# Two heads of scattered gate cells, in place of one, sent behind the first gathered expert rows

## The reference, cut to what matters

```
s1, s2 = scores of the query against two lists of 128 keys, per head (8 heads)
v1, i1 = top_k(s1, 16);  v2, i2 = top_k(s2, 16)
top_s, pos = top_k(all 256 sums, 16);  idx = i1 * 128 + i2   # one of 16384 experts
gate = softmax(top_s)
act  = gelu(x . expert_u[idx])
out += (gate * act) @ expert_v[idx]
```

## Time and profile before

| | us |
|---|---|
| median of 3 runs | 4127.82 (4125.06 to 4128.35) |
| the profiled execution | 4125.72 |
| its span in the trace | 4123.9 |
| PE busy | 3736.4 (91%) |
| DVE busy | 2646.7 (64%) |
| POOL busy | 1887.1 (46%), of it L2147 scatters 416.5 (256 of them) |

### The profile page before, as it was taken

The page is one execution under the profiler, slowest core; times in us unless marked ns, Lnnn a source line. Parts: engine busy times, 40 slices in busy tenths (PEclk is TensorE's granted clock), DMA queues, the critical chain, the costliest instruction groups (busy, mean ns, idle before and its releaser), DMA issues. The chain is left out here.

```text
span 4123.9 us, 42872 instructions
## 1 busy us (share of the span) xinstructions
PE 3736.4 (91%) x15498; PEld 2761.5 (67%) x15498; DVE 2646.7 (64%) x5548; ACT 749.7 (18%) x1387; POOL 1887.1 (46%) x1714
## 2 busy tenths in 40 slices
PE   8889999987899999995798899999878999999947
PEld 7546788876566666652685467888766666666516
DVE  4666214848777677776857662158387777768777
ACT  2244302211100000000222433022110000000002
POOL 6101102777555554566571011027775554555564
PEclk9889999998999999997897899999989999999978
DMA  3301144549999999999623011445499999999996
GB/s 106 113 21 45 52 141 139 143 113 309 408 409 408 409 396 410 403 409 407 239 84 113 31 42 56 141 138 143 111 328 409 409 404 409 404 410 407 404 398 238
DMA packets 331938, 1047.14 MB, mean 254 GB/s; under 512 B 78928, under 2 KB 95952, under 8 KB 312784
## 3 DMA queue, kind: packets, MB, share of 16 engines
q0 software_dynamic: 184320, 537.08, 35.6%
q1 hardware_dynamic: 130352, 488.45, 31.3%
q10 hardware_dynamic: 17056, 18.88, 1.3%
HBM read 1008.49 MB, written 35.78 MB: 253 GB/s over the span
## 5 line engine op out<-in xcount | busy, mean ns | idle before, releaser
L1681 PE MATMUL bank<-v_tile,shared 128*128 128x512 f32 x2048 | 906.4, 597 | 41.3 <-DVE shared L2075 39.0
L2137 POOL DMA_INDIRECT u_rows<-in_peer_u,idx_all x512 | 667.6, 1304 | 525.0 <-DVE act_u L2032 421.8
L2044 DVE SCALAR_TENSOR_TENSOR x<-v_rows,act_w,x 128x1024 f32<-128x1024 f32 x512 | 657.7, 1285 | 354.8 <-DMA v_rows<-in_peer_v,idx_all 313.8
L2137 POOL DMA_INDIRECT v_rows<-in_peer_v,idx_all x512 | 566.6, 1107 | 382.7 <-DVE x L2044 286.0
L2032 DVE CUSTOM_DVE_ANT_0 u_rows<-u_rows,h 128x1024 f32<-128x1024 f32 x512 | 610.4, 1221 | 190.3 <-DMA u_rows<-in_peer_u,idx_all 181.6
L1681 PEld LDWEIGHTS bank<-v_tile,shared 128*128 128x128 f32 x2048 | 391.6, 192 | 494.8 <-issue 444.9
L2147 POOL DMA_INDIRECT first_cells<-first_gate,cell_all x256 | 416.5, 1627 | 590.2 <-DVEq L2024 471.0
L1669 PE MATMUL bank<-hT,bT 128*128 128x256 f32 x2048 | 452.5, 379 | 0.0
L1669 PEld LDWEIGHTS bank<-hT,bT 128*128 128x128 f32 x2048 | 388.4, 190 | 72.0 <-issue 22.0
L1573 PE MATMUL bank<-hT,ring 128*128 128x256 f32 x1536 | 340.6, 383 | 14.3 <-PEq L150 14.2
L1315 POOL TENSOR_TENSOR dn_ct<-dn_lt,mixer_consts 128x512 f32<-128x512 f32 x48 | 64.1, 1336 | 602.9 <-ACT dn_lt L1127 466.5
(11 more groups left out here) (399 smaller groups left out, 4693.7 us busy)
## 6 DMA issues: line engine op xcount, KB each, us to landing
v_tile<-in_peer_v SPq DMA_DIRECT2D x256, 512.0 KB
ring<-in_w_in_panels SPq DMA_DIRECT2D x76, 1024.0 KB
bT<-in_peer_ut SPq DMA_DIRECT2D x128, 512.0 KB
ring<-in_peer_w_query SPq DMA_DIRECT2D x32, 1024.0 KB
aT<-in_peer_ut SPq DMA_DIRECT2D x64, 512.0 KB
sT<-in_peer_ut SPq DMA_DIRECT2D x64, 512.0 KB
first_cells<-zeros SPq DMA_DIRECT2D x16, 1024.0 KB, 12.1
ring<-in_w_abv SPq DMA_DIRECT2D x16, 1024.0 KB
```

The lines of the kernel that those rows point to most:

```text
L1681: ins = mm(acc[t][part][:, :], act_pair[p % AHEAD][:, at:at + P], v_tile[:, e % DENSE, part * 512:part * 512 + 512], start=(e == 0), stop= ...
L2044: stt(out=m.x[:, 2 + t, :], in0=vr[:, n % RINGS, :], scalar=act_w[:, p % 4, i:i + 1], in1=m.x[:, 2 + t, :], op0=ALU.mult, op1=ALU.add).the ...
L2137: nc.gpsimd.indirect_dma_start(out=rows[:, n % RINGS, :], out_offset=None, in_=table, in_offset=bass.IndirectOffsetOnAxis(ap=idx_all[:, t, ...
```

## The change

A constant says how many heads are kept back until the first fetches are out; it was one and is two. So columns 0 to 95 go ahead of the first fetches, and columns 96 to 127 behind them, eight with each of c = 0 to 3 in place of four.

```
+LATE_HEADS = 2
...
-            late = TOPK * (PEER_HEADS - 1)
+            late = TOPK * (PEER_HEADS - LATE_HEADS)
+            late_step = TOPK * LATE_HEADS // LATE_CHUNKS
             for n in range(late):
                 scatter(n)
...
                 if c < LATE_CHUNKS:
-                    for n in range(TOPK // LATE_CHUNKS):
-                        scatter(late + c * TOPK // LATE_CHUNKS + n)
+                    for n in range(late_step):
+                        scatter(late + c * late_step + n)
```

## The result

| | before | after |
|---|---|---|
| median, same chip, 6 runs each | 4126.44 (4124.03 to 4130.29) | 4141.70 (4140.29 to 4144.93) |
| ratio, 95% interval | | 1.0037 (1.0027 to 1.0048) |
| profiled execution / span | 4125.72 / 4123.9 | 4140.41 / 4138.6 |

The account below looks back on a forecast made before the run. The prediction took DMA transfers to bound the dense phase, with gaps ahead of it. Gains of 4.5 us (layer 0) and 1.5 us (layer 1) took the profiled 4125.72 to 4119.7, hence a median of 4122 us, range 4103 to 4136.

Parts of the forecast that it names:

- Step 1: On POOL, the first gather of each layer goes out 24.7 us earlier in layer 1, 24.8 us in layer 0.
- step 2: On DVE, the 16.19 us wait at chunk 0 and small waits go, near 18.7 us a layer.
- Step 3: On POOL before fetch u21, 16 added scatters at 1.93 us cost 30.9 us; u21 leaves unchanged or up to 2 us late.
- Step 4: Behind the last scatter, a shorter DMA queue lets it land in 5 us; SP released 1.9 and 5.5 us earlier.
- Step 5: What reaches the end through PE and the DMA backlog: gains of 4.5 us in layer 0, 1.5 us in layer 1.
- Step 6: Other waits: at columns 96 and 112 POOL finds the earlier scatters landed, so no added wait.
- C: Rival, chance 0.18: added scatters at 2.5 us delay the last scatter and SP's release; each layer loses 5 us, 4138.
- B: Rival, chance 0.14: lead carries through in part, by POOL's saved collisions and the DMA backlog, 9 us a layer, 4110.
- A: Rival, chance 0.08: the lead carries through, about 16 us a layer, 4096.

## Why the prediction was wrong

*Step 1* (first gather 24.7 us earlier) and *step 2* (DVE's wait goes) held: t0 + 0.34 for a forecast of t0 + 0.5, no wait at chunk 0, `hot` 31 ahead by 20 us in both layers (the last mask now stands at t0 + 73.6 in each) for 18 to 19. The run without head 6 shows that this lead is worth 19 to 21 us a layer.

*Step 3* (POOL's stretch) held in kind, and its price was low. I took 1.93 us for an added scatter and it was 2.14, with 34.2 us for 30.9. The difference of 3.3 us is nearly all of u21's lateness in layer 1, 3.6 us. I had written that no surcharges come, having looked at the first of a group, and for gathers at DVE's products; for scatters I looked only beside masks, and there at one row of 1.57, where the mean is 1.69. Groups of eight reach the products, where one takes 2.12.

*Step 4* (last scatter into a short queue, SP earlier by 1.9 and 5.5 us) held in its sum, 2.4 and 5.4 from t0, but by luck: the last scatter's issue ended 3.1 and 3.5 us later than I had it, and the landing took 1.5 us, for which I had taken 5. The two errors cancel.

*Step 5* (what passes on, a gain of 4.5 and 1.5 us) is the one that failed. It had three parts. "In layer 0 PE waited for that load, so it gains": PE then waited for ACT, 29.80 us, and started 5.4 us late (t0 + 153.1 for 147.7). "These go out as before but land into a shorter queue": the queue was short, and for that reason SP's release fell on u21 itself; its 4 MB halved the rate at which rows came and made the choice 5.3 us later. The run that holds SP back shows this part: there the 5.3 us are gone.

"Less some 1.5 us in which the queue runs dry": I had the lead in bytes about right (1.3 MB or 3.2 us at t0 + 120, forecast 2.5 to 7 us), but the DMA engines then moved 4.7 MB less than before in layer 1 from t0 + 120 to t0 + 180, 11.6 us at 0.407, and 4.3 MB less in layer 0. The engines had nothing to carry since nearly every source was held by one of two things: SP's queue by the last scatter, and then PE, DVE and POOL (10.16 us for a buffer at 3123.35) by the head choice behind chunk 5. Before, neither hole was there. The late store of the last gates had a small part in that, 0.82 MB of the 4.7 and nothing after t0 + 140; the rest is 2.25 MB of SP's loads and 1.6 MB of gathers, which then came in time. Moving the loads and products of `pre` 10 and 11 out from behind both things (both edits on the kernel after) gives some 20 us back.

*Step 6* (waits at columns 96 and 112 are over by then) held. The DVE wait for u17, 5 to 12 by forecast, was 16.73.

*The rivals.* C, slower, was right in sign, time (4138 for 4141.7) and its first link: a price near 2.2 us, u21 "over 4 us late" (3.6 and 5.3 against t0). Its second link, that SP's release slips, was wrong; SP was early and did harm. So its 0.18 was too little, and for a reason I had before me: POOL full from t0 to u21 with 30.4 us of room for 30.9 of work leaves no place for an error in one direction only. B's backlog was there (1.3 MB ahead at t0 + 120) and was lost again. A is what the run without head 6 does.

What stays open: whether and why both edits on the kernel after end some 5 us ahead of both on the kernel before. The ratios, 0.9989 and 1.0001, have intervals that overlap (0.9980 to 0.9998 and 0.9991 to 1.0011), and in the profiled executions the difference lies ahead of t0 of layer 0, which comes at 901.77 and 905.83; from t0 to the last fetch the two take 1128.3 and 1124.8 against 1128.5 and 1123.8 us. It is not shown which of the remaining short stretches (249 and 310 GB/s) could be filled further.

## What to carry to other kernels

When the phase that follows is at the limit of the DMA engines, ask of a change ahead of it what keeps each queue supplied in every 20 us until then, and count bytes, not the start of a product: the same two edits, which shorten TensorE's stall at `pre` 10, were worth 0 and 3 us a layer here where the DMA queues were full (and the 3 had another source), and 7 and 11 us where they ran empty. Work moved out of a stall must not be put ahead of what other queues wait for: the change stopped costing time only when the loads and products behind the last scatter were moved away from it. And an indirect DMA is priced beside what VectorE does at its new place.

## What the hardware showed that I had not expected

- In the stretch of the kernel after (layer 1), a scatter of 128 values costs GpSimd 1.54 us beside an idle VectorE, 1.67 beside one-hot masks (`tensor_scalar` and `tensor_tensor` mixed) and 2.12 beside products with two inputs (up to 2.48; up to 3.21 in the kernel before).
- Its landing was quick: from the end of the last issue to SP's next instruction 1.46 and 1.55 us with a short queue, where I had read 3.87 us at the turn of a head and 7.4 to 12.3 us behind a backlog.
- A burst of 4 MB from SP's queue spaces the gathers of GpSimd's queue 2.56 us apart in place of 1.29, at an unchanged 412 GB/s in all.
